# A decoder layer on one core: the stages before the experts rewritten

## What is computed

```python
mod = silu(c) @ w_ada + b_ada          # 1024 -> 6 x 1024
shift_m, scale_m, gate_m, shift_f, scale_f, gate_f = split(mod, 6)

h = rms_norm(x, norm_mix_pre) * (1 + scale_m) + shift_m
u = h @ w_in                           # 1024 -> xa 512, ga 512, xb 512
xa = causal_depthwise_conv(xa, conv_w, conv_b)          # 4 taps
r = sigmoid(xa @ gate_a (8 blocks) + gate_a_b); i = sigmoid(xa @ gate_x + gate_x_b)
a = exp(-8 r softplus(-lam)); ya = scan(a, sqrt(1 - a*a) * i * xa) * gelu(ga)
yb = ((window means of xb, 2 4 8 16) - xb) @ pool_w + pool_b, times pool_scale
x = x + gate_m * rms_norm([ya, yb] @ w_out, norm_mix_post)

h = rms_norm(x, norm_ffn_pre) * (1 + scale_f) + shift_f
top_val, top_idx = top_k(h @ router_w + router_b, 4); gates = softmax(top_val)
f = sum over the 4 of gates * (clamped_swiglu(h @ w1[e] + b1[e]) @ w2[e] + b2[e])
x = x + gate_f * rms_norm(f, norm_ffn_post)
```

## Time and profile before

| | |
|---|---|
| median of 3 runs | 1527.55 us |
| the profiled execution, its own time | 1541.51 us |
| its span, first to last instruction | 1539.5 us |
| TensorE busy | 1247.8 us (81%) |
| VectorE, ScalarE, GpSimd busy | 405.4, 219.3, 281.8 us |
| DMA | 464.22 MB, mean 302 GB/s |
| chain that ended last | PE 67%, DMA 17%, DVE 5%, SPq 5% |

### The profile page before, as it was taken

The page is one execution under the profiler, slowest core; times in us unless marked ns, Lnnn a source line. Parts: engine busy times, 40 slices in busy tenths (PEclk is TensorE's granted clock), DMA queues, the critical chain, the costliest instruction groups (busy, mean ns, idle before and its releaser), DMA issues.

```text
span 1539.5 us, 28706 instructions
## 1 busy us (share of the span) xinstructions
PE 1247.8 (81%) x9039; PEld 433.3 (28%) x9040; DVE 405.4 (26%) x826; ACT 219.3 (14%) x482; POOL 281.8 (18%) x431
## 2 busy tenths in 40 slices
PE   3796799444899899988675899997699989999961
PEld 1342345321233233322111233322132223322320
DVE  2111323511223222222110222221032222222317
ACT  2103443200010111110100111111011111100101
POOL 4041000021022212221110121221021211211212
PEclk9797899567999999998876899998799999999975
DMA  9509351419955958899999993559999998899354
GB/s 302 221 2 380 137 218 42 177 63 417 416 215 204 420 228 335 343 393 420 421 419 421 419 420 136 210 217 419 420 378 398 390 419 333 330 420 420 145 196 195
DMA packets 77917, 464.22 MB, mean 302 GB/s; under 512 B 11967, under 2 KB 12071, under 8 KB 29761
## 3 DMA queue, kind: packets, MB, share of 16 engines
q1 hardware_dynamic: 49280, 314.72, 50.5%
q10 hardware_dynamic: 17520, 126.12, 19.9%
q0 software_dynamic: 11088, 22.99, 4.5%
HBM read 454.34 MB, written 16.91 MB: 306 GB/s over the span
## 4 chain that ended last, share of the span: by engine, by line
PE 67%; DMA 17%; DVE 5%; SPq 5%; issue 3%; ACT 2%; POOLq 1%; POOL 1%; ACTq 0%; DVEq 0%
PE bank L1347 32%; PE bank L1375 17%; DMA W<-in_expert_w 11%; PE bank L1253 5%; SPq L366 4%; DMA W<-in_w_ada 4%; PE bank L1299 4%; PE bank L1356 2%; PE bank L1426 2%; PE bank L1221 1%; PE bank L1335 1%; DVE W L1183 1%; DVE OV L1105 1%; PE bank L1269 1%; DMA OV<-h_rows,src_cur 1%
## 5 line engine op out<-in xcount | busy, mean ns | idle before, releaser
L1347 PE MATMUL bank<-W,OV 128*32 128x512 f32 x5056 | 574.1, 607 | 48.2 <-DMA W<-in_expert_w 37.8
L1375 PE MATMUL bank<-W,OV 128*32 128x512 f32 x2528 | 325.9, 661 | 45.9 <-ACT OV L779 22.7
L1347 PEld LDWEIGHTS bank<-W,OV 128*32 128x32 f32 x5056 | 158.4, 111 | 438.6 <-issue 378.2
L1105 DVE TENSOR_TENSOR OV<-bank,OV 128x512 f32<-128x512 f32 x79 | 54.6, 692 | 491.7 <-PE bank L1347 486.2
L1375 PEld LDWEIGHTS bank<-W,OV 128*32 128x32 f32 x2528 | 84.7, 118 | 232.2 <-issue 193.2
L1118 DVE COPY OV<-bank 64x512 f32<-64x512 f32 x79 | 54.7, 693 | 305.0 <-PE bank L1375 305.0
L562 POOL DMA_INDIRECT OV<-h_rows,src_cur x104 | 106.0, 1019 | 62.0 <-POOL src_cur L557 42.6
L557 POOL COPY src_cur<-OV 128x2 int32 (+1 forms) x52 | 11.6, 223 | 493.2 <-PE bank L1335 493.2
L774 ACT ACTIVATE OV<-OV 128x256 f32<-128x256 f32 x79 | 35.1, 444 | 463.0 <-DVE OV L1107 403.0
L1356 PE MATMUL bank<-ident,store 128*128 128x128 f32 x216 | 48.9, 315 | 48.7 <-DVE store L1113 43.8
L1253 PE MATMUL bank<-W 128*128 128x512 f32 x192 | 85.7, 606 | 1.1 <-ACT W L683 1.0
(11 more groups left out here) (228 smaller groups left out, 693.4 us busy)
## 6 DMA issues: line engine op xcount, KB each, us to landing
W<-in_expert_w SPq DMA_DIRECT2D x252, 1024.0 KB
W<-in_expert_w ACTq DMA_DIRECT2D x120, 1024.0 KB
W<-in_w_ada SPq DMA_DIRECT2D x24, 1024.0 KB, 7.7
W<-y_rows SPq DMA_DIRECT2D x4, 2048.0 KB, 14.7
W<-in_w_in SPq DMA_DIRECT2D x3, 2048.0 KB, 12.3
W<-in_w_out SPq DMA_DIRECT2D x1, 4096.0 KB, 20.5
store<-in_x SPq DMA_DIRECT2D x4, 512.0 KB, 5.9
h_rows<-W POOLq DMA_DIRECT2D x4, 512.0 KB, 3.4
```

The source lines that it names most:

```text
L1105: TTo(u_sb[:, hf, :], bank[hf][:, :], b1_cur, ALU.add).then_inc(u_ok[hf], 1)
L1347: last = mm(bank[hf][H * j:H * j + H, :], xT[:, hf, k % QM, H * (k // QM):H * (k // QM) + H], W1[:, slot, k, UW * j:UW * j + UW], start=(k ...
L1375: last = mm(bank[4 + hf][H * j:H * j + H, :], gT[:, hf, r, H * c:H * c + H], W2[:, c, r, HW * piece:HW * piece + HW], start=(c == 0), stop ...
```

## The change

Only the stages before the experts are rewritten.

- Modulation: products of 512 columns, the strips now hold two column halves of two row slices; `sel2` picks and adds the strips. Biases and gains lie in two partitions instead of in 32 each. Bias and gain of vectors 0 and 1 come by column, with the small vectors, of which there are ten loads now.
- The pieces of vectors 2 to 5 come after the groups of `xa` and `xb`, two after each. SP starts w_ada without waiting for the small vectors, and loads w_out before piece 11.
- The pool products come before the last gate part. The first two `mix` groups leave the product that needs the last scan to the end.
- Routing is done per token tile; the rank products of tiles 0 to 2 stand before the last logits. The two tables are made by column, and the table product follows column by column. Counts and gates are made after them.
- GpSimd's fills come earlier, the first gather comes before the two empty scatters. TensorE reads its registers before the first transposes. `b1_all` serves as a row of gains first and is loaded later.

```diff
@@ SP
-            sp.wait_ge(vec_in, 8 * 16)
             for n in range(2 * PIECES):
                 load_ada(n)
             load_win(0, 0)
             load_win(2, 1)
-            for n in range(2 * PIECES, 3 * PIECES):
+            for n in range(2 * PIECES, 2 * PIECES + ADA_RING):
+                load_ada(n)
+            sp.dma_start(w_out_sb, w_out_v).then_inc(wout_in, 16)
+            for n in range(2 * PIECES + ADA_RING, 4 * PIECES + 2):
                 load_ada(n)
             sp.wait_ge(prod, number["xa", FT - 1] + 1)
             load_win(1, 0)
-            sp.dma_start(w_out_sb, w_out_v).then_inc(wout_in, 16)
-            for n in range(3 * PIECES, 6 * PIECES):
+            for n in range(4 * PIECES + 2, 6 * PIECES):
                 load_ada(n)
...
@@ GpSimd
+            pool.wait_ge(prod, number["mix", TT - 1, 1] + 1)
+            link(nc.gpsimd.memset(xg[0], 0.0))
+            link(nc.gpsimd.memset(xg[1], 0.0))
...
             pool.wait_ge(idx_ok, 1)
-            link(nc.gpsimd.memset(xg[0], 0.0))
-            link(nc.gpsimd.memset(xg[1], 0.0))
...
+            gather(0)
             for hf in range(2):
                 scatter(hf, 0, NOTHING)
-            gather(0)
...
@@ VectorE
+            def route_tile(i):
+                dve.wait_ge(evac, number["logits", i] + 1)
...
+                link(TTo(logits[:, i, :], logits[:, i, :], router_bias, ALU.add))
+                link(nc.vector.max(top[:, i, :], logits[:, i, :]))
+                link(nc.vector.max_index(top_i[:, i, :], top[:, i, :], logits[:, i, :]))
+                chosen = tk_f[:, 0, i * TOPK:(i + 1) * TOPK]
+                link(nc.vector.tensor_copy(chosen, top_i[:, i, 0:TOPK]))
+                link(TTo(hot_e[:, i, :, :], over(iota_e, 1, P, TOPK, E), over(chosen, 2, P, TOPK, E), ALU.is_equal))
+                nc.vector.reduce_sum(sel[:, i, :], hot_e[:, i, :, :].rearrange("p k e -> p e k"), axis=AX.X)\
+                    .then_inc(sel_ok, 1)
...
-            link(TTo(hot_t, over(iota_t, 1, P, TK, P), over(tk_f[:, 3, :], 2, P, TK, P), ALU.is_equal))
-            link(TTo(slot_val, over(iota_q, 1, P, TK, NQ), over(tk_f[:, 2, :], 2, P, TK, NQ), ALU.is_equal))
-            TTo(slot_val, slot_val, over(tok_no, 2, P, TK, NQ), ALU.mult).then_inc(slots_ok, 1)
+            for n in range(TK):
+                TS(hot_t[:, n, :], iota_t, tk_f[:, 3, n:n + 1], None, ALU.is_equal).then_inc(slots_ok, 1)
+                TS(slot_val[:, n, :], iota_q, tk_f[:, 2, n:n + 1], tok_no[:, n:n + 1], ALU.is_equal, ALU.mult)\
+                    .then_inc(slots_ok, 1)
...
@@ TensorE
+            def mod_piece(n):
+                v, kk = n // (KT // AK), n % (KT // AK)
+                if v >= 2 and kk == 0:
+                    pe.wait_ge(mod_row, v - 1)
+                pe.wait_ge(ada_in[n % ADA_RING], 16 * (n // ADA_RING + 1))
+                for k in range(AK):
+                    for half in range(N2):
+                        g = N2 * k + half
+                        last = mm(bank[6 + v % 2][H * g:H * g + H, :], c_rep[:, kk * AK + k, :],
+                                  ada_ring[:, n % ADA_RING, k, HW * half:HW * half + HW], start=(kk == 0),
+                                  stop=(kk == KT // AK - 1))
+                last.then_inc(ada_used, 1)
...
+            piece = 2 * PIECES
+            for name, slot in (("xa", 0), ("xb", 1)):
+                for _ in u_part(name, slot, 1):
+                    mod_piece(piece)
+                    mod_piece(piece + 1)
+                    piece += 2
...
+            first = [ready(("mix", 0, n)) for n in range(2)]
+            FIRST_KS = list(range(FT, KT)) + list(range(FT - 1))
+            for n in range(2):
+                mix(0, n, first[n], FIRST_KS)
+            pe.wait_ge(bc_ok, 2)
+            spread_row(2)
             pe.wait_ge(gel_ok, FT)
+            for n in range(2):
+                mix(0, n, first[n], [FT - 1]).then_inc(prod, 1)
...
+                if what == ("logits", TT - 1):
+                    pe.wait_ge(route_const, 5)
+                    pe.wait_ge(bc_ok, 6)
+                    pe.wait_ge(sel_ok, TT - 1)
+                    for to in range(TT - 1):
+                        for b in range(to + 1):
+                            rank_add(to, b)
+                    for b in range(TT - 1):
+                        rank_add(TT - 1, b)
+                        total_add(b)
```

More of the change, by code:

```diff
@@ L140, in hybrid_layer @@
         gel = take(T)
+        router_bias = take(E)
         B_HI = B_hi.shape[1]
@@ L212, in hybrid_layer @@
         for f in range(FT):
+            if f == FT - 1:
+                order += [("pool", g) for g in range(FT)]
             order += [("r", f), ("i", f), ("ga", f)]
-        order += [("pool", f) for f in range(FT)]
         for i in range(TT):
@@ L1285, in _, with spread_row @@
-            pe.wait_ge(wout_in, 16)
-            pe.wait_ge(gel_ok, FT)
-            pe.wait_ge(evac, number["pool", FT - 1] + 1)
+            def spread_row(v):
+                for half in range(N2):
+                    last = mm(bank[4 + 2 * (v % 2) + half][:, :], sel2[:, half:half + 1].to_broadcast([P, P]),
+                              ada_rows[:, v, :], start=True, stop=True)
+                last.then_inc(bc_ps, 1)
+            pe.wait_ge(mod_row, 6)
+            spread_row(0)
+            spread_row(1)
@@ L1288, in _, with total_add @@
+            def total_add(b):
+                return mm(bank[5][:, 0:E], ones[:, :], sel[:, b, :], start=(b == 0), stop=(b == TT - 1))
             pe.wait_ge(router_in, 32)
-            for what in order[number["mix", 0, 0]:]:
+            for what in order[number["mix", 0, 1] + 1:]:
                 i = what[1]
+                if what == ("logits", TT - 1):
[8 more added lines that the diff above has]
+                        total_add(b)
@@ L1296, in _ @@
                 if what[0] == "mix":
[L1297 to L1300 removed]
+                    last = mix(i, what[2], ps, list(range(FT, KT)) + list(range(FT)))
                 elif what[0] == "hT":
```

320 lines of the change are left out of this document (159 added, 161 removed).

## The result

The changed kernel takes **1488.43 us**, the median of 4 runs (1486.98 to 1493.22); the kernel before, 1529.3 us over its 4 (1525.8 to 1534.59). The ratio is **0.9735, 95% interval [0.9697, 0.9773]**. The forecast was 1466 (1454 to 1481): the direction is right, the time lies 22 us above it and 7 us above the range.

What follows compares the result with a forecast made beforehand. It took TensorE's waits before the experts, chiefly for w_ada pieces (42.8 us), as the bound, with the expert stage shifting whole. Gains of 61.5 us, scaled to 61, off 1527.55 gave 1466.5, called 1466 (1454 to 1481).

Steps and rivals of the forecast that it cites:

- Sum: Whole part before the experts: gains of 50.4, 2.2, 2.3, 5.8 and 0.8 give 61.5 us, scaled by 0.991, off 1527.55.
- I charge 2 us: Input products: TensorE waits 2 us for w_ada piece 11, wanted at 60.8 and landing near 63 behind w_out's load.
- the start at 42: First input product: starts near 42 us (39 to 45), before 55.58, with piece 7 issued near 27.5.
- The register reads: Ahead of the first expert product: TensorE reads registers before the transposes, saving 0.8 of 7.1 us.
- a gain of 2.2 in routing: End of the last mix group to the counts: 25.2 us instead of 27.4, with rank products ahead of logits 3.
- the tables' stage: Counts to index tables: 16.7 us instead of 19.0, a gain of 2.3 (bounds -0.3 and 4.3).
- rival A: Gates: ScalarE keeps its old 10.6 us a group instead of 9.1, stage 48 instead of 37.9; 1476 us, chance 0.13.
- B: Routing gives nothing: the 32 small operations cost full length, rank products lie on the path; 1471 us, chance 0.10.
- C: Input products: w_ada pieces late at every pair, 2 us at seven more pairs; 1480 us, chance 0.10.
- D: Better than forecast: piece 7 by 31, no stall at piece 11, table at 6.3; 1458 us, chance 0.13.
- E: Slower than before: alternating wide and strip products hold TensorE's clock low, 161 us more; 1627 us, chance 0.03.
- other rule: Index tables: each VectorE operation waits for an empty pipe, so the 32 cost full length; gain -0.3 us.

Runs made afterwards that it cites:

- the second comparison: The changed kernel run once more with no edit, beside the kernel before on the same chip: 1487.67 us, ratio 0.9706.

## Why the prediction was right and where it was wrong

**The error of 22 us has two parts.** *The base.* I took the gain between events of one profile, 61.5 us, and subtracted it from the median of runs, 1527.55, after scaling by 0.991. The profile it was read from took 1541.5, 14 us more, and the scaling took off 0.5. But those 14 us were no general slowness that a factor takes out. The median over 74 later runs of the kernel before is 1534.1: the profiled execution lay 7.4 above it, near the slowest of all, and the median of three runs 6.6 below. The second profile of the same program had 6 us less in the first part and 1 in the rest; part of what I counted as won was not there in the median run. Against the profile's own time the sum gives 1541.5 - 61.5 = 1480.0, against the measured 1488.43. *The terms.* Between the two profiles the start of the experts moved by 54.9, not by 61.5: 6.6 us of the forecast's mechanism are missing. The expert stage was 0.6 longer, and the median lies 1.4 above the profiled execution. With the base, 14, these are the 22 us. Beside the kernel before on the same chip the change gained 41 us at first and 45 in the second comparison, by the ratios, with 61 forecast. That before's spread lies in the rewritten part rests on two profiles and on the runs' spread (before's lie 12 to 17 us apart, those of the changed kernel and its versions 2 to 7, though over fewer runs); against it stand the 9 us by which the expert stage alone differs between profiles.

**The steps that failed** are two. The larger is in "Sum": a gain read in one execution, taken off the median of others; it is worth 14 of the 22 us. The other, in the mechanism, is "I charge 2 us" for piece 11, and with it the start at 42. The wait is 6.2, the low clock behind it, which I had not charged, 1.9, the start 3.4 late; the input products end 9.1 later than forecast. Splitting the load gave back 8.0. Part of it is a slip in the sum itself: from the first input product to the wait there are two groups and three pieces, 14.3 + 2.8 = 17.1 us (measured 45.37 to 62.44), not 18.8, so that its own landing at 63 meant a wait of 3.9. And the landing was too early: I let 12.6 MB start at 29 at 0.40 MB/us; but piece 7, which these bytes stand behind, went out at 30.84 (3.3 later than the 27.5 assumed), and from 30 to 45 the engines moved 331 GB/s, not 400. By these numbers piece 11 lands at about 67.5, an estimate; it was used at 68.67. The small-row loads made the start late by 2.5 of the 3.4; but that didn't matter for the end, as held back they changed nothing. I had two terms where there was one, the landing of piece 11.

**The register reads** were undersized: 0.8 against 2.0, with 2.3 more that went for a reason left open. It pays back part of the loss.

**The rank products.** I forecast a gain of 2.2 in routing, and 2.5 were measured; right, but the run with them behind the logits shows that the whole stage could have given 6.1, and that this part of the change costs 3.6. I had worked out the cost (24 x 0.22) and taken it as given. The terms that I name for this stage add up to 24.6, not 25.2; the taking out of the logits between them has no term. In the tables' stage the upper bound of the gain is 4.0, not 4.3, by the 6.3 of the table product.

**Right:** the first w_ada product (13.3, 13.07); gates (37.9, 38.3), with ScalarE's four groups taking 37.1 us (126.29 to 166.09 less 2.7 for the pool evacuations), 9.3 each with the first table load, instead of 10.6, so rival A didn't come; the first `mix` groups (19.6, 20.15); the order of gates behind the 32 small operations and their cost (16.7, 16.5); the earlier gather (its copy 0.2 after the index tables, though it then took 5.5 to the transposes instead of 4.6), and the expert stage of 1203.

**The rivals.** B didn't come: routing gained what was forecast, though the rank products were on the path, as B had it and the forecast too. C came at one place only; there are no waits at the seven other pairs. D failed by piece 7, used at 35.94 and not by 31, and by the stall at piece 11. E, the clock, didn't come: 0.96 to 1.00 from 45 to 230. The Trainium skill, TensorEngine Tiling (Array Packing), Key Properties, warned of a drain at each change of mode; here the pairs of pieces between wide groups take 1.92 without a gap, so none shows.

## What to carry to other kernels

A gain summed between events of one profile holds for that profile: take it off its own time, and take a second profile of the same program before scaling to a median, above all when the part to be rewritten is where executions differ. A large load in the queue of a small ring can hold up the ring's next load wherever it stands whole (6.2 and 6.9 us here for 4 MB); cut it to the ring's size and put it behind pieces. And before work is pulled ahead to "fill a gap", ask whether the instruction behind it is the one that the next engine waits for: the rank products fitted, but into the wrong gap.

## What the runs showed of the hardware

- DMA engines at share 1.0 moved 244 GB/s while short rows were being loaded and 384 with these held back, in the same 8 us of the same program. Share alone doesn't tell how much more an order of loads can give.
- VectorE's small operations, where none reads what the one before wrote, start every 0.20 and 0.26 us though each takes longer (VectorE's timeline of the changed kernel):

```profile
261.34 0.29 DVE L1094 TENSOR_SCALAR W<-OV 128x128 f32<-128x128 f32 x1
261.53 0.35 DVE L1095 TENSOR_SCALAR W<-OV 128x132 f32<-128x132 f32 x1
261.79 0.29 DVE L1094 TENSOR_SCALAR W<-OV 128x128 f32<-128x128 f32 x1
```

  The 32 took 7.4 us instead of the 10.3 that their durations add up to. The Trainium skill, VectorE: DVE Perf Modes, The DRAIN you can't avoid, gives the rule that the next operation waits for the empty pipe, and says that one which isn't held starts earlier. The trace shows the earlier start for these; the forecast's "other rule" had left that exception out.
- A reduction that reads 512 inputs per partition for 128 outputs took 1.02 us (`G`, L1113 in the changed kernel), one of as many inputs for 16 outputs 0.69 (L1088).
